# Layer norms of a decoder trunk: row sum taken from the residual addition, variance from a Square on ACT, centred product in PSUM, and the two blocks of the last norm interleaved

## Chip, cores and metric

One core of one Trainium2 chip. The metric is the device time of one execution in microseconds (us). The kernel before has a median of 1365.14 us over three runs (1364.58 to 1365.68).

## The reference, cut to what matters

Two layers over 256 tokens of width 1024, all in float32. Every sublayer is followed by a post-norm residual; there are four of them, numbered 0 to 3 here:

```python
def layer_norm(x, g, b):
    mu = jnp.mean(xf, axis=-1, keepdims=True)
    xc = xf - mu
    var = jnp.mean(xc * xc, axis=-1, keepdims=True)
    y = xc * lax.rsqrt(var + LN_EPS) * g + b

# layer 0
x = layer_norm(DEEP_ALPHA * x + deltanet_mixer(x, ...), ...)         # norm 0
x = layer_norm(DEEP_ALPHA * x + dense_swiglu(x, ...), ...)           # norm 1
# layer 1
x = layer_norm(DEEP_ALPHA * x + sliding_window_mixer(x, ...), ...)   # norm 2
x = layer_norm(DEEP_ALPHA * x + moe_swiglu(x, ...), ...)             # norm 3, the output
```

The last sublayer sends each token to its two best of 8 experts and adds the two results with their weights.

## The kernel before, in words

The 256 tokens are two blocks of 128 (`b` = 0 and 1), one token per partition: the residual `x` is a tile of 128 x 2 x 1024 in SBUF. All large products are made of three float32r matmuls, so every weight unit of 128 x 2048 is first split: SyncE loads it into a ring `raw` of 6 slots, ACT rounds it into `hi` (`cut_hi`, L519), DVE subtracts to get `lo` (`cut_lo`, L832), and TensorE uses it and increments `unit_used`. `hi` and `lo` are rings of 3, so ACT's cut of unit j waits until unit j-3 was used (`AHEAD` = 3). The order of work on each engine is written out by hand, and each engine carries its instructions out in that order; semaphores are all that ties the engines together.

A norm sits between two stages. TensorE ends the projection of block 0 (`block0_done`), then that of block 1 (`unit_used`), into PSUM banks 0 to 3 (norms 0 and 2) or 4 to 7 (norm 1). DVE runs `norm` (L845) for block 0, then for block 1:

```python
step(dve.scalar_tensor_tensor(x = ALPHA * x + ps))                     # L853
link(dve.bn_stats(...)) ; link(dve.bn_stats(...))                      # L857
step(dve.bn_aggr(...)) ; dve.tensor_scalar(lnve = var + 1e-5)          # L859, L860 -> ln_var
step(dve.scalar_tensor_tensor(x = (x - mean) * lng))                   # L864
dve.wait_ge(ln_rstd, ...)                                              # the power -0.5 on POOL, L387
dve.scalar_tensor_tensor(x = x * lnrs + lnb)                           # L867 -> ln_done[b]
```

`step` makes DVE wait for its own instruction, `link` only counts it, `settle` waits for all counted so far. POOL takes `lnve` to the power -0.5 (L387) and, when both blocks of a norm are done, loads the next `lng` and `lnb` (L359, L360). TensorE waits for `ln_done[b]` and transposes the block (`turn_x`, L1286, in `turn`, L1283) into banks 4 to 7; ACT rounds the transposes into `xT_hi` (`turn`, L531, copy at L529), DVE makes `xT_lo` (L842), and the next projection begins.

While this goes on, ACT has only the cuts of the weight units ahead: in norm 0 those of `U_OUT + u + AHEAD` (L664), in norm 1 of `U_DOWN + u + AHEAD` (L681), in norm 2 of `U_O + u + AHEAD` (L740); then it runs `turn`. In norm 2 it also cuts the router weights and issues the DMA that stores each finished block to `xs` in HBM (L748).

Norm 3 comes after the experts. ACT copies the last expert's result out of PSUM and stores it; POOL gathers the two rows of every token with four indirect DMAs (L500) into `picked`; DVE adds them to `x` with four `scalar_tensor_tensor` (L1264: two for block 0, two for block 1) and only then runs `norm(3, None)`, without L853, block 0 and then block 1. SyncE writes each block out once `ln_done[b]` has come (L330). TensorE has nothing left to do there, and after the experts ACT has no work either.

Of the kernel before, what the change touches and what calls it, by code (L numbers as in the profile page):

```python
# [17 lines left out]
ALU = mybir.AluOpType  # L18
# [7 lines left out]
P = 128  # L26
# [6 lines left out]
AHEAD = 3  # L33


def trunk(nc, x_in, w_in, conv_w, a_log, dt_bias, norm_w, w_out, w_kv, w_q, sinks, w_o, w_gu, w_down,
# [39 lines left out]
    with ctx:  # L76
        def sb(name, shape, dt=F32, where=None):
            return (where or ctx).enter_context(nc.sbuf_tensor(name, shape, dt))
# [15 lines left out]
        bnst = sb("bnst", [P, NB, 2, 6])  # L94
        bnmv = sb("bnmv", [P, NB, 2])
# [109 lines left out]
        ln_var, ln_rstd, ln_done = sem("ln_var"), sem("ln_rstd"), [sem(f"ln_done{b}") for b in range(NB)]  # L205
# [312 lines left out]
        def _(act):  # L518
# [16 lines left out]

            act.dma_start(wab[:, :, :], w_in[0][:, QKV * P + D:].rearrange("(k p) n -> p k n", p=P)).then_inc(wab_here, 16)
# [127 lines left out]
            for u in range(4):  # L664
                cut_hi(U_OUT + u + AHEAD)
            turn(2)

# [13 lines left out]
            for u in range(FC):  # L681
                cut_hi(U_DOWN + u + AHEAD)
            turn(3)

# [55 lines left out]
            for u in range(1, 4):  # L740
                cut_hi(U_O + u + AHEAD)
# [7 lines left out]
            turn(4)  # L749
            act.wait_ge(w2_arg, 1)  # L750
# [60 lines left out]
            with act.If(full > P):  # L811
                experts(1)

# [3 lines left out]
        def _(dve):  # L817
# [27 lines left out]
            def norm(i, bank, last=None):  # L845

                for b in range(NB):
                    if bank is not None:
                        if b == 0:
                            dve.wait_ge(block0_done, i + 1)  # L850
                        else:
                            used(last)
                        step(dve.scalar_tensor_tensor(out=x[:, b, :], in0=x[:, b, :], scalar=ALPHA,  # L853
                                                      in1=ps[:, bank + 2 * b:bank + 2 * b + 2, :].rearrange("p b n -> p (b n)"),
                                                      op0=ALU.mult, op1=ALU.add))
                    for q in range(2):
                        link(dve.bn_stats(bnst[:, b, q, :], x[:, b, 512 * q:512 * q + 512]))  # L857
                    settle()
                    step(dve.bn_aggr(bnmv[:, b, :], bnst[:, b, :, :].rearrange("p q s -> p (q s)")))  # L859
                    dve.tensor_scalar(lnve[:, b:b + 1], bnmv[:, b, 1:2], 1e-5, None, ALU.add).then_inc(ln_var, 1)  # L860
                    if b == 0:
                        dve.wait_ge(ln_here, 32 * (i + 1))

                    step(dve.scalar_tensor_tensor(out=x[:, b, :], in0=x[:, b, :], scalar=bnmv[:, b, 0:1], in1=lng[:, :],  # L864
# [842 lines left out]
```

## Time and profile before

| | |
|---|---|
| median of three runs | 1365.14 us |
| lowest, highest | 1364.58, 1365.68 us |
| the profiled execution's own time | 1365.49 us |
| its span in the trace | 1363.7 us |
| busy in the span | PE 93%, PEld 80%, DVE 73%, ACT 60%, POOL 6% |

The span is what the trace covers, from the first instruction to the last. The busy shares are averages over the whole kernel, most of which is the expert stage; what a norm is worth has to be read from the stretch of that norm. PE is TensorE, PEld its weight loads, DVE VectorE, ACT ScalarE, POOL GpSimd, SP SyncE.

### The profile page before, as it was taken

How to read it: one execution, taken by the hardware profiler on the slowest of the kernel's cores; microseconds unless marked ns; L12 is line 12 of the kernel's file. 1: busy time of each engine (PE TensorE's matmuls, PEld its weight loads, DVE VectorE, ACT ScalarE, POOL GpSimd, SP SyncE). 2: the span in 40 equal slices, each digit the busy share in tenths (PEclk: the TensorE clock that was granted, in tenths of full speed). 3: DMA queues.
4: the chain of work that ended last, by engine and by line, in shares of the span. 5: the costliest groups of instructions: out<-in, count | busy, mean ns of one | idle time of the engine just before them, and what ended most of it. 6: DMA issues, size and time to landing. Idle time of an engine off the chain costs nothing.

```text
span 1363.7 us, 18999 instructions
## 1 busy us (share of the span) xinstructions
PE 1262.0 (93%) x6973; PEld 1093.5 (80%) x6973; DVE 1001.4 (73%) x835; ACT 820.7 (60%) x800; POOL 88.2 (6%) x111
## 2 busy tenths in 40 slices
PE   5999988999998977799999999999999999999990
PEld 5997986999986965588888788887788888888880
DVE  4876845455547475388888798888788888888883
ACT  4884342344442463177777777777777777777760
POOL 3033211100002001000000000000000000000001
PEclk8999998999998989599999999999899999999995
DMA  9744011955564423399999999999999999999963
GB/s 315 215 146 133 1 32 62 314 183 185 185 203 146 145 90 105 114 326 367 385 381 353 378 363 379 390 387 343 357 371 382 387 383 353 383 402 373 385 239 110
DMA packets 186522, 366.55 MB, mean 269 GB/s; under 512 B 12192, under 2 KB 69648, under 8 KB 186416
## 3 DMA queue, kind: packets, MB, share of 16 engines
q1 hardware_dynamic: 179744, 345.02, 70.6%
q0 software_dynamic: 4080, 14.80, 3.2%
q10 hardware_dynamic: 2592, 5.36, 1.0%
q8 instruction: 62, 1.02, 0.3%
q14 instruction: 44, 0.36, 0.1%
HBM read 354.65 MB, written 10.49 MB: 268 GB/s over the span
## 4 chain that ended last, share of the span: by engine, by line
PE 86%; DVE 7%; ACT 3%; issue 2%; POOL 1%; DMA 1%; POOLq 0%; SPq 0%; ACTq 0%; DVEq 0%
PE ps L1272 83%; PE ps L1630 1%; DVE lo L834 1%; POOL lnrs L387 1%; DVE conv L895 1%; DVE bnst L857 1%; DVE x L867 1%; DVE xT_lo L842 1%; ACT hi L523 1%; DVE x L853 1%; ACT sS L705 1%; PE ps L1623 0%; DMA picked<-ys,row 0%; DMA x<-in_x 0%; DVE x L1264 0%
## 5 line engine op out<-in xcount | busy, mean ns | idle before, releaser
L834 DVE TENSOR_TENSOR lo<-raw,hi 128x2048 fp32r<-128x2048 f32 x327 | 747.1, 2298 | 197.1 <-ACT hi L523 196.1
L523 ACT ACTIVATE hi<-raw 128x2048 fp32r<-128x2048 f32 x327 | 627.3, 1919 | 363.1 <-PE ps L1272 353.6
L1272 PE MATMUL ps<-hi,xg_hi 128*128 128x512 f32 x704 | 280.8, 399 | 11.0 <-issue 6.3
L1272 PE MATMUL ps<-hi,xg_lo 128*128 128x512 f32 x704 | 276.7, 393 | 0.0
L1272 PE MATMUL ps<-lo,xg_hi 128*128 128x512 f32 x704 | 276.7, 393 | 0.0
L1272 PE MATMUL ps<-xT_hi,hi 128*128 128x256 f32 x624 | 179.9, 288 | 1.3 <-DVE xT_lo L842 1.3
L1272 PE MATMUL ps<-xT_lo,hi 128*128 128x256 f32 x624 | 178.8, 287 | 0.0
L1272 PE MATMUL ps<-xT_hi,lo 128*128 128x256 f32 x624 | 178.7, 286 | 0.0
L1272 PEld LDWEIGHTS ps<-hi,xg_hi 128*128 128x128 f32 x704 | 133.8, 190 | 40.3 <-issue 12.3
L1272 PEld LDWEIGHTS ps<-hi,xg_lo 128*128 128x128 f32 x704 | 133.8, 190 | 28.8
L1272 PEld LDWEIGHTS ps<-lo,xg_hi 128*128 128x128 f32 x704 | 134.0, 190 | 26.9
L1272 PEld LDWEIGHTS ps<-xT_hi,hi 128*128 128x128 f32 x624 | 122.2, 196 | 2.1 <-issue 2.0
L1272 PEld LDWEIGHTS ps<-xT_lo,hi 128*128 128x128 f32 x624 | 122.1, 196 | 0.1
L1272 PEld LDWEIGHTS ps<-xT_hi,lo 128*128 128x128 f32 x624 | 122.1, 196 | 0.0
L1272 PE MATMUL ps<-hi,hE_hi 128*128 128x512 f32 x352 | 110.5, 395 | 0.0
L1272 PE MATMUL ps<-hi,hE_lo 128*128 128x512 f32 x352 | 108.6, 390 | 0.0
L1272 PE MATMUL ps<-lo,hE_hi 128*128 128x512 f32 x352 | 108.5, 389 | 0.0
L1272 PEld LDWEIGHTS ps<-lo,hE_hi 128*128 128x128 f32 x352 | 66.1, 188 | 13.9
L1272 PEld LDWEIGHTS ps<-hi,hE_lo 128*128 128x128 f32 x352 | 66.1, 188 | 13.9
L1272 PEld LDWEIGHTS ps<-hi,hE_hi 128*128 128x128 f32 x352 | 64.3, 188 | 12.1
L482 POOL DMA_INDIRECT xg<-xs,idx x8 | 7.6, 954 | 580.1 <-PE ps L1623 564.4
L895 DVE SCALAR_TENSOR_TENSOR conv<-ps,cw,conv 128x255 f32<-128x255 f32 (+2 forms) x72 | 29.1, 474 | 17.1 <-ACT conv L553 17.1
(270 smaller groups left out, 1244.4 us busy)
## 6 DMA issues: line engine op xcount, KB each, us to landing
raw<-in_moe_w_gu SPq DMA_DIRECT2D x352, 512.0 KB, 6.9
raw<-in_moe_w_down SPq DMA_DIRECT2D x176, 512.0 KB, 5.9
raw<-in_ffn_w_gu SPq DMA_DIRECT2D x44, 512.0 KB, 4.7
raw<-in_dn_w_in SPq DMA_DIRECT2D x32, 512.0 KB, 7.9
raw<-in_ffn_w_down SPq DMA_DIRECT2D x22, 512.0 KB, 4.3
raw<-in_dn_w_out SPq DMA_DIRECT2D x8, 512.0 KB, 4.0
ys<-oneh POOLq DMA_DIRECT2D x1, 4096.0 KB, 16.4
raw<-in_sw_w_q SPq DMA_DIRECT2D x8, 512.0 KB, 4.0
```

The lines of the kernel that those rows point to most:

```text
L387: return pool.tensor_tensor(dst, src, mhalf[:, 0:src.shape[1]], ALU.pow)
L482: pool.indirect_dma_start(xg[:, :], None, xs, bass.IndirectOffsetOnAxis(ap=idx[:, p, e:e + 1], axis=0)).then_inc(gathered, 16)
L523: act.activation(slot(hi, j), slot(raw, j), ACT.Copy).then_inc(hi_ready, 1)
L705: act.activation(s, s, ACT.Exp, bias=nmax[:, st, b, i:i + 1], accum_out=ssum[:, st, b, i:i + 1])
L834: dve.tensor_tensor(slot(lo, j), slot(raw, j), slot(hi, j).bitcast(F32), ALU.subtract).then_inc(lo_ready, 1)
L842: dve.tensor_tensor(xT_part(xT_lo, s), ps[:, 4 + s, :].rearrange("p (k t) -> p k t", k=4), xT_part(xT_hi, s).bitcast(F32), ALU.subtract).t ...
L853: step(dve.scalar_tensor_tensor(out=x[:, b, :], in0=x[:, b, :], scalar=ALPHA, in1=ps[:, bank + 2 * b:bank + 2 * b + 2, :].rearrange("p b n ...
L857: link(dve.bn_stats(bnst[:, b, q, :], x[:, b, 512 * q:512 * q + 512]))
L867: dve.scalar_tensor_tensor(out=x[:, b, :], in0=x[:, b, :], scalar=lnrs[:, b:b + 1], in1=lnb[:, :], op0=ALU.mult, op1=ALU.add).then_inc(ln_ ...
L895: dve.scalar_tensor_tensor(out=conv[:, t, d:T], in0=ps[:, t % 4, 0:T - d], scalar=cw[:, w:w + 1], in1=conv[:, t, d:T], op0=ALU.mult, op1=A ...
L1272: return pe.matmul(dst, lhsT, rhs, start=start, stop=stop)
L1630: last = pe.transpose(ps[:, 6 + c % 2, m * P:(m + 1) * P], actE[:, c % 2, m * P:(m + 1) * P], ident[:, :])
```

## The change

The statistics of a norm are computed in another way. The residual addition also writes out its row sum (`accum_out`), from which DVE makes `lnmu32` = -mean/32 and `lnmu` = mean. ACT computes the Square of x/32 - mean/32 over 1024 columns with a sum, which is the variance (`lnvr`; the squares themselves go to a PSUM region that nobody reads), and adds 1e-5 (`lnve`). POOL's power stays. The centred product goes to PSUM, to the banks of the block's own projection, and the last instruction reads it from there. In ACT's order `deviation` is put between the cuts, before `turn`; one cut of each stage moves to behind `turn`. In norm 3 the additions of the gathered rows become part of `norm`, and the steps of the two blocks alternate.

```diff
+        ln_mean, ln_square = sem("ln_mean"), sem("ln_square")
...
+            def deviation(i, b, bank):
+                act.wait_ge(ln_mean, 2 * i + b + 1)
+                act.activation(ps[:, bank + 2 * b:bank + 2 * b + 2, :].rearrange("p b n -> p (b n)"), x[:, b, :], ACT.Square,
+                               scale=1.0 / 32, bias=lnmu32[:, b:b + 1], accum_out=lnvr[:, b:b + 1]).then_inc(ln_square, 1)
+                act.wait_ge(ln_square, 2 * i + b + 1)
+                act.activation(lnve[:, b:b + 1], lnvr[:, b:b + 1], ACT.Copy, bias=1e-5).then_inc(ln_var, 1)
...
-            for u in range(4):
-                cut_hi(U_OUT + u + AHEAD)
+            cut_hi(U_OUT + 0 + AHEAD)
+            cut_hi(U_OUT + 1 + AHEAD)
+            deviation(0, 0, 4)
+            cut_hi(U_OUT + 2 + AHEAD)
+            deviation(0, 1, 4)
             turn(2)
+            cut_hi(U_OUT + 3 + AHEAD)
...
-            for u in range(FC):
+            for u in range(FC - 2):
                 cut_hi(U_DOWN + u + AHEAD)
+            deviation(1, 0, 0)
+            cut_hi(U_DOWN + FC - 2 + AHEAD)
+            deviation(1, 1, 0)
             turn(3)
+            cut_hi(U_DOWN + FC - 1 + AHEAD)
...
-            for u in range(1, 4):
-                cut_hi(U_O + u + AHEAD)
+            cut_hi(U_O + 1 + AHEAD)
+            deviation(2, 0, 4)
+            cut_hi(U_O + 2 + AHEAD)
+            deviation(2, 1, 4)
...
             turn(4)
+            cut_hi(U_O + 3 + AHEAD)
...
+            for b in range(NB):
+                deviation(3, b, 4)
...
             def norm(i, bank, last=None):
-                for b in range(NB):
+                def pair(bank, b):
+                    return ps[:, bank + 2 * b:bank + 2 * b + 2, :].rearrange("p b n -> p (b n)")
+                def mean(b):
                     if bank is not None:
...
+                        step(dve.scalar_tensor_tensor(out=x[:, b, :], in0=x[:, b, :], scalar=ALPHA, in1=pair(bank, b),
+                                                      op0=ALU.mult, op1=ALU.add, accum_out=lnsum[:, b:b + 1]))
+                    else:
+                        dve.wait_ge(picked_here[b], 32)
+                        step(dve.scalar_tensor_tensor(out=x[:, b, :], in0=picked[:, b, 0, :], scalar=gw[:, b, 2:3],
+                                                      in1=x[:, b, :], op0=ALU.mult, op1=ALU.add))
+                        step(dve.scalar_tensor_tensor(out=x[:, b, :], in0=picked[:, b, 1, :], scalar=gw[:, b, 3:4],
+                                                      in1=x[:, b, :], op0=ALU.mult, op1=ALU.add, accum_out=lnsum[:, b:b + 1]))
+                    dve.tensor_scalar(lnmu32[:, b:b + 1], lnsum[:, b:b + 1], -1.0 / (32 * D), None, ALU.mult).then_inc(ln_mean, 1)
+                    step(dve.tensor_scalar(lnmu[:, b:b + 1], lnsum[:, b:b + 1], 1.0 / D, None, ALU.mult))
-                    for q in range(2):
-                        link(dve.bn_stats(bnst[:, b, q, :], x[:, b, 512 * q:512 * q + 512]))
-                    settle()
-                    step(dve.bn_aggr(bnmv[:, b, :], bnst[:, b, :, :].rearrange("p q s -> p (q s)")))
-                    dve.tensor_scalar(lnve[:, b:b + 1], bnmv[:, b, 1:2], 1e-5, None, ALU.add).then_inc(ln_var, 1)
+                def centre(b):
                     if b == 0:
                         dve.wait_ge(ln_here, 32 * (i + 1))
-                    step(dve.scalar_tensor_tensor(out=x[:, b, :], in0=x[:, b, :], scalar=bnmv[:, b, 0:1], in1=lng[:, :],
+                    link(dve.scalar_tensor_tensor(out=pair(bank or 0, b), in0=x[:, b, :], scalar=lnmu[:, b:b + 1], in1=lng[:, :],
                                                   op0=ALU.subtract, op1=ALU.mult))
+                def finish(b):
+                    settle()
                     dve.wait_ge(ln_rstd, 2 * i + b + 1)
-                    dve.scalar_tensor_tensor(out=x[:, b, :], in0=x[:, b, :], scalar=lnrs[:, b:b + 1], in1=lnb[:, :],
+                    dve.scalar_tensor_tensor(out=x[:, b, :], in0=pair(bank or 0, b), scalar=lnrs[:, b:b + 1], in1=lnb[:, :],
                                              op0=ALU.mult, op1=ALU.add).then_inc(ln_done[b], 1)
+                mean(0)
+                centre(0)
+                if bank is None:
+                    mean(1)
+                    finish(0)
+                else:
+                    finish(0)
+                    mean(1)
+                centre(1)
+                finish(1)
...
             dve.wait_ge(x_scaled, 1)
-            for b in range(NB):
-                dve.wait_ge(picked_here[b], 32)
-                for i in range(2):
-                    step(dve.scalar_tensor_tensor(out=x[:, b, :], in0=picked[:, b, i, :], scalar=gw[:, b, 2 + i:3 + i],
-                                                  in1=x[:, b, :], op0=ALU.mult, op1=ALU.add))
             norm(3, None)
```

## Rows read from the trace of the kernel before

**Rows 1.** The page: its span, and the chain that ended last, by engine.
```profile
span 1363.7 us, 18999 instructions
...
PE 86%; DVE 7%; ACT 3%; issue 2%; POOL 1%; DMA 1%; POOLq 0%; SPq 0%; ACTq 0%; DVEq 0%
```

**Rows 2.** Stretches: length, then busy us (instructions) per engine, PE clock, DMA share, GB/s.
```profile
224.93:237.00 12.07, 6.67 (x33) 5.17 (x32) 10.84 (x15) 4.80 (x4) 3.04 (x2) 0.92 0.26 86
...
1332.00:1363.70 31.70, 0.00 (x0) 0.00 (x0) 13.30 (x16) 0.93 (x1) 6.81 (x6) 0.53 0.32 117
```

**Rows 3.** Timeline of norm 0: start, us, engine, line, operation, shapes [idle before <-releaser].
```profile
224.93 1.22 DVE L853 SCALAR_TENSOR_TENSOR x<-x,ps 128x1024 f32<-128x1024 f32 x1 [1.14 <-PE ps L1272]
...
230.43 1.91 ACT L523 ACTIVATE hi<-raw 128x2048 fp32r<-128x2048 f32 x1 [0.80 <-PE ps L1272]
230.81 1.21 DVE L853 SCALAR_TENSOR_TENSOR x<-x,ps 128x1024 f32<-128x1024 f32 x1
...
233.62 0.15 DVE L860 TENSOR_SCALAR lnve<-bnmv 128x1 f32<-128x1 f32 x1
...
233.85 1.52 POOL L387 TENSOR_TENSOR lnrs<-lnve,mhalf 128x1 f32<-128x1 f32 x1 [4.35 <-DVE lnve L860]
235.48 1.28 DVE L867 SCALAR_TENSOR_TENSOR x<-x,lnrs,lnb 128x1024 f32<-128x1024 f32 x1 [0.51 <-POOL lnrs L387]
...
236.82 1.97 PE L1283 MATMUL ps<-ident,x 128*128 128x128 f32 x8 [4.78 <-DVE x L867]
```

**Rows 4.** Timeline of norm 2: the last instruction of block 1.
```profile
540.63 1.28 DVE L867 SCALAR_TENSOR_TENSOR x<-x,lnrs,lnb 128x1024 f32<-128x1024 f32 x1 [0.87 <-POOL lnrs L387]
```

**Rows 5.** Groups by form: line, engine, operation, shapes, count | busy us, mean ns | idle.
```profile
L853 DVE SCALAR_TENSOR_TENSOR x<-x,ps 128x1024 f32<-128x1024 f32 x6 | 7.3, 1218 | 3.4 <-PE ps L1272 3.4
...
L867 DVE SCALAR_TENSOR_TENSOR x<-x,lnrs,lnb 128x1024 f32<-128x1024 f32 x8 | 10.3, 1284 | 4.5 <-POOL lnrs L387 4.5
...
L1264 DVE SCALAR_TENSOR_TENSOR x<-picked,gw,x 128x1024 f32<-128x1024 f32 x4 | 5.1, 1284 | 18.1 <-DMA picked<-ys,row 18.0
...
L529 ACT ACTIVATE ysb<-ps 128x1024 f32<-128x1024 f32 x8 | 8.1, 1007 | 6.2 <-PE ps L1272 6.2
...
L529 ACT ACTIVATE qT<-ps 128x256 f32<-128x256 f32 x8 | 2.6, 377 | 10.6 <-PE ps L1272 10.6
...
L705 ACT ACT_TABLE_LOAD x1 | 1.3, 1283 | 0.0
...
L707 ACT ACTIVATE ske<-ske 128x8 f32<-128x8 f32 x4 | 0.8, 194 | 0.0
```

**Rows 6.** Timeline: an Exp with a sum on ACT, and a hand-over from DVE to ACT.
```profile
484.26 0.50 ACT L705 ACTIVATE sS<-sS,nmax 128x256 f32<-128x256 f32 x1
484.66 0.19 ACT L705 ACTIVATION_READ_ACCUMULATOR sS<-sS,nmax 128x1 f32 x1
...
553.38 0.16 DVE L1161 TENSOR_TENSOR gw<-m 128x2 f32<-128x2 f32 x1
...
553.58 0.21 ACT L751 ACTIVATE gw<-gw 128x2 f32<-128x2 f32 x1 [9.00 <-DVE gw L1161]
```

**Rows 7.** Timeline of DVE and ACT just after norm 0.
```profile
240.07 4.48 DVE L834 TENSOR_TENSOR lo<-raw,hi 128x2048 fp32r<-128x2048 f32 x2
...
248.10 1.92 ACT L523 ACTIVATE hi<-raw 128x2048 fp32r<-128x2048 f32 x1 [8.67 <-PE ps L1272]
```

**Rows 8.** Timeline of the end of the kernel, norm 3.
```profile
1345.97 5.25 DVE L1264 SCALAR_TENSOR_TENSOR x<-picked,gw,x 128x1024 f32<-128x1024 f32 x4 [17.98 <-DMA picked<-ys,row]
1351.26 1.29 DVE L857 BATCH_NORM_STATS2 bnst<-x 128x6 f32<-128x512 f32 x2
...
1356.02 4.96 SPq L330 DMA_DIRECT2D out<-x  x2
...
1357.70 1.52 POOL L387 TENSOR_TENSOR lnrs<-lnve,mhalf 128x1 f32<-128x1 f32 x1 [3.10 <-DVE lnve L860]
1359.32 1.28 DVE L867 SCALAR_TENSOR_TENSOR x<-x,lnrs,lnb 128x1024 f32<-128x1024 f32 x1 [0.51 <-POOL lnrs L387]
```

More of the change, by code:

```diff
@@ L93, in trunk @@
         mhalf = sb("mhalf", [P, NB * H])
-        bnst = sb("bnst", [P, NB, 2, 6])
-        bnmv = sb("bnmv", [P, NB, 2])
+        lnvr = sb("lnvr", [P, NB])
+        lnsum = sb("lnsum", [P, NB])
+        lnmu = sb("lnmu", [P, NB])
+        lnmu32 = sb("lnmu32", [P, NB])
         lnve = sb("lnve", [P, NB])
@@ L204, in trunk @@
         turned, turn_hi, turn_lo = sem("turned"), sem("turn_hi"), sem("turn_lo")
-        ln_var, ln_rstd, ln_done = sem("ln_var"), sem("ln_rstd"), [sem(f"ln_done{b}") for b in range(NB)]
+        ln_mean, ln_square, ln_var, ln_rstd, ln_done = sem("ln_mean"), sem("ln_square"), sem("ln_var"), sem("ln_rstd"), [sem(f"ln_done{b}") for b in range(NB)]
         conv_step, tap_ready, silu_done = sem("conv_step"), sem("tap_ready"), sem("silu_done")
@@ L852, in norm @@
                             used(last)
-                        step(dve.scalar_tensor_tensor(out=x[:, b, :], in0=x[:, b, :], scalar=ALPHA,
-                                                      in1=ps[:, bank + 2 * b:bank + 2 * b + 2, :].rearrange("p b n -> p (b n)"),
-                                                      op0=ALU.mult, op1=ALU.add))
-                    for q in range(2):
-                        link(dve.bn_stats(bnst[:, b, q, :], x[:, b, 512 * q:512 * q + 512]))
-                    settle()
```

## The prediction

> **What bounds the kernel now.** I read the page first: TensorE holds 86% of the chain that ended last, DVE 7% [rows 1]. So only stretches in which TensorE stands still can give time back, and every norm is one. The stretches by stage come next [rows 2]: the 12.07 us of norm 0 hold 6.67 us of PE work, which lies in their first half, while DVE is busy for 10.84. The last 31.7 us hold no PE work at all, and DVE has the most there, 13.30. Then the timeline of norm 0 [rows 3]. Block 0's addition starts at 224.93, while TensorE is still on block 1. Block 1's starts at 230.81 with no idle time before it, although ACT, released by TensorE, shows that block 1's product was ready by 230.43: DVE, not TensorE, sets that start. From there one chain runs to the transposes at 236.82: addition, statistics, power on POOL, last instruction, 6.0 us in all. Norms 1 and 2 have the same form. In the end stretch [rows 8] the same chain runs twice in a row, behind four additions on DVE, and the output leaves behind it.
>
> **Norms 0 to 2: the statistics.** Before, POOL starts 233.85 - 230.81 = 3.04 us after the addition's start [rows 3]. I build the same distance for the new chain:
> - The addition, 1.22 [rows 5]. Its sum must be read out, for which DVE shows no row. Bounds: nothing (hidden under the pipeline), or a small DVE instruction of its own, 0.15 [rows 3]. I take 0.08, since such an instruction overlaps its predecessor on ACT by half [rows 6].
> - 0.03 for DVE's wait for itself, 0.15 for `lnmu32` [rows 3], 0.04 to hand over to ACT (553.38 + 0.16 to 553.58) [rows 6]. `lnmu` comes after it and lies beside ACT.
> - The Square over 1024 columns. Lower end 1.01, the copy of 1024 columns [rows 5]. Upper end: an Exp with a bias per partition and a sum takes 0.50 for 256 columns [rows 6] where a copy takes 0.38 [rows 5], so 1.01 + 0.12 = 1.13. I take 1.12, since it has bias and sum. The read of the sum starts 0.10 before its end and takes 0.19 [rows 6]: 0.09 more. Together 1.21, between 1.10 and 1.22.
> - 0.03 for ACT's wait for itself, 0.20 for `lnve` (a small ACT instruction, 0.19 [rows 5] to 0.21 [rows 6]), and 0.08 to POOL (233.62 + 0.15 to 233.85) [rows 3].
>
> Sum: 1.22 + 0.08 + 0.03 + 0.15 + 0.04 + 1.21 + 0.03 + 0.20 + 0.08 = 3.04, with ends 2.84 and 3.12. So the chain stays as long as it was: what DVE saves in two BATCH_NORM_STATS2 comes back as a Square with two hand-overs. Per block the difference is 0.0 (-0.2 to +0.1), and six blocks are in a row on the path (block 0 delays block 1, since DVE sets its start): 0.0, between -1.2 and +0.5.
>
> The **Trainium skill** (VectorE: DVE Perf Modes, "Two Vector instructions with no wait between them") says that an op which also writes its accumulator is two instructions. By that the read-out is certainly there, but no row here prices it.
>
> **Centred product in PSUM.** The last instruction then reads PSUM. The addition with its PSUM source takes 1218 ns and the last instruction with none 1284 [rows 5], but the first also has a constant for its scalar where the other reads one per partition. So I take 1.28 for both new forms; the end below is 1.22 for each last instruction, -0.06 for six blocks, -0.4. The centring lies under the wait for POOL: it now starts some 0.1 later and still ends over 1 us before the power does.
>
> **Queues passed.** On ACT block 0's `deviation` comes before the third cut, which TensorE releases about 2.8 us after the addition's start; it is about over by then, so that cut moves by a few tenths. Block 1's comes before `turn`, so block 0's `xT_hi` copies move back by some 1.5 us, to before DVE wants them (behind its last instruction). The fourth cut (230.43) moves to after `turn`, to about 239.4 to 241.4. DVE's second subtraction behind `turn` wants it 2.2 us into the pair that starts at 240.07 [rows 7], some 0.9 later; TensorE wants it after two more units, and the first is only used up at 248.10 [rows 7]. Cost 0. Without that cover it would be up to 1.9 per norm (the cut). Norm 1 is alike. In norm 2 the fourth cut comes before the small Exp of the routing, but only just behind `turn`, which has 6 us and more before that Exp. The store of block 0 to `xs` is queued behind block 1's `deviation`, but the gathers wait for both stores, and block 1's stays where it is. SyncE refills `raw` when `lo` is made, in DVE's unchanged order; POOL's loads of `lng` wait for the same `ln_done`. Nothing moves.
>
> One accident: in norm 2 block 1's last instruction sat idle for 0.87 us before it [rows 4] where 0.51 is usual [rows 3]. I can't tell what of; if it goes, -0.36.
>
> **Norm 3.** Before: additions at 1345.97 (1.32 each with their waits), statistics at 1351.26, last instruction of block 1 1359.32 to 1360.60 [rows 8]. After, with the durations above:
> - Block 0's two additions end at 1348.57, its `lnmu32` starts at 1348.71; `lnmu`, then the centring from 1348.95 to 1350.23.
> - Block 1's additions follow from 1350.15; the second ends at 1352.75 and `lnmu32` starts at 1352.86.
> - Block 0's power is over at 1348.71 + 0.15 + 0.04 + 1.21 + 0.03 + 0.20 + 0.08 + 1.53 = 1351.95, hidden under those additions. Its last instruction runs 1353.1 to 1354.4, centring of block 1 to 1355.6.
> - Block 1's power ends at 1352.86 + 1.71 + 1.53 = 1356.10; hand-over 0.1 (233.85 + 1.52 to 235.48) [rows 3]; last instruction 1356.2 to 1357.5.
>
> So 1360.6 - 1357.5 = 3.1 us, with ends of 2.8 and 3.5 by the bounds. The first output transfer starts at about 1354.4 instead of 1356.02, the second 3.1 us behind it; from the last instruction's end to the end of the span it was 1363.7 - 1360.6 = 3.1, and I leave that.
>
> **Sum.** 1365.49 (the profiled execution) - 3.1 - 0.0 = 1362.4. That execution lies 0.35 above the median of 1365.14, so for a median: **1362.0**. 0.2% is 2.7 us, about what a measurement can tell here from no change.
>
> **Rivals.**
> - **A, the statistics get shorter too (0.15).** The lower ends (Square near 1.01, read-outs hidden, PSUM reads at 1.22) and the stall of norm 2 gone: 0.1 to 0.2 per block. For it: every bound is of this trace. Time 1361.0.
> - **B, the summing addition runs slower (0.07).** The four additions of `picked` read both tensors from SBUF at 1284 ns for 1024 columns [rows 5], and none writes a sum. If a sum cost such an instruction its rate, the two that make one would take about 1.07 more each, and both are on the path in norm 3: 2.1 of 3.1 lost, 1364.1. In norms 0 to 2 one tensor is in PSUM, so nothing changes there. The Trainium skill (Vector Engine (DVE) Microarchitecture Reference, "Points that are easy to get wrong") says that a scalar_tensor_tensor with two non-bf16 SBUF sources halves throughput, none being left for the accumulator. The rows show no halving without a sum; whether there is one with it no row tells.
> - **C, Square is not in the table that Exp leaves behind (0.08).** Elsewhere Square follows Silu, with no load of its own; in norm 2 it follows the Exps, loaded at L705, 1283 ns a load [rows 5]. A load in front of block 0's Square is 1.3 on the path; the one back for the routing's Exp lies mostly beside TensorE's work. Time 1363.4.
> - **D, the detour over ACT is longer than the sum says, and the kernel is slower (0.02).** ACT would wait until the Square's writes have landed before the sum can be read and handed on. It is on the path six times in norms 0 to 2; in norm 3 it eats into the 3.1 only once (block 0's is hidden for 1.1 us). It decides from 3.1 / 7 = 0.44 us per block on; at 0.9 it gives 1362.0 + 6.3 = 1368.3. Against it: the read of a sum starts 0.10 before its Exp ends [rows 6].
> - That the change doesn't do what it says is hardly open: the interleaved order is in DVE's own queue.
>
> **How the numbers follow.** The forecast has 0.68, A 0.15, B 0.07, C 0.08, D 0.02. The forecast's own range is 1361.3 to 1362.9 (0.5 either way for six small terms, 0.3 for norm 3). For 8 in 10 I take A in and reach to C: 1360.8 to 1363.6. Faster by over 0.2% means under 1362.4: A, and about two thirds of the forecast, 0.60. Same: its rest, B and C, 0.38. Slower: D, 0.02.
>
> **What would show it.** Right: POOL's power starts 2.9 to 3.1 us after each addition's start; norms 0 to 2 keep their 6.0 us from block 1's addition to the transposes; in the end stretch no idle time on DVE before block 0's last instruction, under 1 us before block 1's, and 11.5 us from the first addition to the last instruction's end instead of 14.6. Wrong: an L523 cut that the subtraction behind `turn` waits for; an ACT_TABLE_LOAD in norm 2; summing additions over 1.5 us; a power that starts over 3.3 us after the addition.

## Result, and the profile after

The changed kernel takes 1356.59 us (median of 6 runs, 1355.35 to 1358.09) beside 1365.35 for the kernel before (6 runs, 1364.58 to 1366.37). The ratio is 0.9936, 95% interval [0.9923, 0.9949]: 8.8 us faster, where 3.1 were forecast. The direction was right, and the time lies well below the range.

The profiled execution took 1356.62. The page of the changed kernel gives the span and the chain, and the stretches of norm 0 and of the end follow in the columns of [rows 2].

```profile
span 1354.8 us, 19018 instructions
...
PE 88%; DVE 5%; ACT 3%; issue 2%; DMA 1%; POOL 1%; POOLq 0%; SPq 0%; ACTq 0%; DVEq 0%
```

```profile
225.16:237.30 12.14, 7.98 (x40) 6.63 (x38) 9.24 (x14) 6.21 (x10) 2.28 (x5) 0.89 0.26 86
1326.00:1354.80 28.80, 0.03 (x1) 0.00 (x0) 10.55 (x14) 3.91 (x7) 6.62 (x6) 0.57 0.36 129
```

DVE's share of the chain falls from 7 to 5%. In norm 0 DVE is busy for 9.24 us in place of 10.84 [rows 2], and ACT, with its two Squares, for 6.21 in place of 4.80.

To find the 8.8 us I cut both spans at the same events: the start of each norm's first addition, and the end of its last instruction. This table is worked out from the timelines of DVE and ACT; "experts" ends where ACT, its last `ysb` copy done, issues that copy's store, and "gathers" ends with the first addition of `picked`.

| part, us | before | after | difference |
|---|---|---|---|
| up to norm 0 | 224.93 | 225.16 | +0.23 |
| norm 0 | 11.83 | 10.38 | -1.45 |
| feed-forward | 186.67 | 185.49 | -1.18 |
| norm 1 | 11.85 | 10.37 | -1.48 |
| attention | 94.43 | 94.48 | +0.05 |
| norm 2 | 12.20 | 10.39 | -1.81 |
| experts | 791.04 | 790.91 | -0.13 |
| gathers | 13.02 | 13.22 | +0.20 |
| norm 3 | 14.63 | 11.32 | -3.31 |
| output | 3.10 | 3.08 | -0.02 |

The sum is -8.90, the difference of the spans. Norm 3 gave what was forecast (3.31 for 3.1). Norms 0 to 2, put at 0.0, gave 4.74. The four norms together make 8.05; of the rest the largest part is the 1.18 of the feed-forward stage, which is taken up again below. The timeline of norm 0 after shows where (start, us, engine, line, operation, shapes, idle before it and its releaser):

```profile
228.17 0.55 POOL L389 TENSOR_TENSOR lnrs<-lnve,mhalf 128x1 f32<-128x1 f32 x1 [25.30 <-ACT lnve L543]
228.82 1.28 DVE L898 SCALAR_TENSOR_TENSOR x<-ps,lnrs,lnb 128x1024 f32<-128x1024 f32 x1 [0.85 <-POOL lnrs L389]
...
230.60 1.22 DVE L878 SCALAR_TENSOR_TENSOR x<-x,ps 128x1024 f32<-128x1024 f32 x1 [0.50 <-PE ps L1309]
231.75 0.08 DVE L878 DVE_READ_ACCUMULATOR x<-x,ps 128x1 f32 x1
231.87 0.15 DVE L886 TENSOR_SCALAR lnmu<-lnsum 128x1 f32<-128x1 f32 x1
...
232.05 1.12 ACT L540 ACTIVATE ps<-x,lnmu 128x1024 f32<-128x1024 f32 x1 [2.16 <-DVE lnmu L886]
232.12 1.29 DVE L892 SCALAR_TENSOR_TENSOR ps<-x,lnmu,lng 128x1024 f32<-128x1024 f32 x1
233.11 0.19 ACT L540 ACTIVATION_READ_ACCUMULATOR ps<-x,lnmu 128x1 f32 x1
233.33 0.20 ACT L543 ACTIVATE lnve<-lnvr 128x1 f32<-128x1 f32 x1
...
233.61 0.55 POOL L389 TENSOR_TENSOR lnrs<-lnve,mhalf 128x1 f32<-128x1 f32 x1 [4.89 <-ACT lnve L543]
234.26 1.28 DVE L898 SCALAR_TENSOR_TENSOR x<-ps,lnrs,lnb 128x1024 f32<-128x1024 f32 x1 [0.85 <-POOL lnrs L389]
```

The new chain from the addition to POOL's start is 233.61 - 230.60 = 3.01 us; it was put at 3.04, and it was 3.04 before [rows 3]. What changed is the instruction behind it. POOL's power, the same operation on the same 128x1 tile, takes 0.55 us where it took 1.52 [rows 3]. From block 1's addition to the end of its last instruction that makes 234.26 + 1.28 - 230.60 = 4.94 us in place of 235.48 + 1.28 - 230.81 = 5.95.

Block 0 gets less of it. Its last instruction starts 3.66 us after its addition where it took 4.68 before, but block 1's addition comes only 5.44 after block 0's instead of 5.88, and now it shows 0.50 us of idle time released by TensorE. Before it had none [rows 3]. Block 0 gives 0.44 and block 1 1.01, together the 1.45 of norm 0.

The end of the changed kernel, in the same columns:

```profile
1340.40 1.28 DVE L882 SCALAR_TENSOR_TENSOR x<-picked,gw,x 128x1024 f32<-128x1024 f32 x1 [18.19 <-DMA picked<-ys,row]
...
1344.50 1.28 DVE L882 SCALAR_TENSOR_TENSOR x<-picked,gw,x 128x1024 f32<-128x1024 f32 x1
...
1344.79 1.42 POOL L389 TENSOR_TENSOR lnrs<-lnve,mhalf 128x1 f32<-128x1 f32 x1 [6.53 <-ACT lnve L543]
1345.82 1.28 DVE L884 SCALAR_TENSOR_TENSOR x<-picked,gw,x 128x1024 f32<-128x1024 f32 x1
...
1348.65 1.28 DVE L892 SCALAR_TENSOR_TENSOR ps<-x,lnmu,lng 128x1024 f32<-128x1024 f32 x1
1348.76 3.33 SPq L332 DMA_DIRECT2D out<-x  x2
1348.89 1.45 POOL L389 TENSOR_TENSOR lnrs<-lnve,mhalf 128x1 f32<-128x1 f32 x1 [2.67 <-ACT lnve L543]
1350.44 1.28 DVE L898 SCALAR_TENSOR_TENSOR x<-ps,lnrs,lnb 128x1024 f32<-128x1024 f32 x1 [0.51 <-POOL lnrs L389]
```

Here the power takes 1.42 and 1.45 again. So its time depends on what runs beside it. Each long power has a DVE instruction that reads two tensors from SBUF, started before the power did, and ends 0.40 to 0.43 us after that instruction's end:

- before, block 1 of norm 0: the centring (233.69, 1.28 us) ends at 234.97, the power (233.85, 1.52) at 235.37;
- after, norm 3: the addition of `picked` 1344.50 + 1.28 = 1345.78, the power 1344.79 + 1.42 = 1346.21; the centring 1348.65 + 1.28 = 1349.93, the power 1348.89 + 1.45 = 1350.34.

In norms 0 to 2 after, the centring is over (232.12 + 1.29 = 233.41) before the power starts at 233.61.

The row of before that shows this best wasn't among the ones I had chosen. It is the centring in block 1 of norm 0:

```profile
233.69 1.28 DVE L864 SCALAR_TENSOR_TENSOR x<-x,bnmv,lng 128x1024 f32<-128x1024 f32 x1
```

### The profile page after: what moved, and what is told of

It is laid out like the page before. It is cut to its first block, busy times and chain, and to the rows that moved or that the text cites. A ratio compares the mean times of both kernels' runs of the same rounds, so it can differ in the third digit from the quotient of the medians.

```text
span 1354.8 us, 19018 instructions
## 1 busy us (share of the span) xinstructions
PE 1261.9 (93%) x6973; PEld 1094.1 (81%) x6973; DVE 991.2 (73%) x827; ACT 831.3 (61%) x824; POOL 82.0 (6%) x111
## 4 chain that ended last, share of the span: by engine, by line
PE 88%; DVE 5%; ACT 3%; issue 2%; DMA 1%; POOL 1%; POOLq 0%; SPq 0%; ACTq 0%; DVEq 0%
PE ps L1309 85%; PE ps L1667 1%; DVE lo L856 1%; DVE conv L937 1%; ACT hi L525 1%; ACT sS L722 1%; PE ps L1320 0%; PE ps L1660 0%; DMA picked<-ys,row 0%; DVE xT_lo L864 0%; DMA x<-in_x 0%; DVE x L898 0%; ACT ps L540 0%; DMA ys<-ysb 0%; ACT ps L574 0%
```

## The experiments

The theory: a power of POOL that starts while DVE works through an instruction with two SBUF inputs is held until that is done (called P or the hold in the expectations); without it the power takes 0.55. The rival: the power waits for what was written by DVE, and is quick when ACT wrote its input (W). Runs of one batch share the runs of before beside them, and those medians lie between 1365.47 and 1366.22.

**1. The kernel before, centring behind the power.** `ln_rstd` is waited for first.

```diff
+                    dve.wait_ge(ln_rstd, 2 * i + b + 1)
                     step(dve.scalar_tensor_tensor(out=x[:, b, :], in0=x[:, b, :], scalar=bnmv[:, b, 0:1], in1=lng[:, :],
                                                   op0=ALU.subtract, op1=ALU.mult))
-                    dve.wait_ge(ln_rstd, 2 * i + b + 1)
```

> Theory P (shared reads): POOL's power takes 1.52 us in the kernel before because DVE's centring, which reads two tensors from SBUF, runs at the same time, and the power cannot read its one input until the centring is over; alone it takes 0.55. Here the centring of the kernel before waits for the power. P expects 0.55 per power in all eight, and a kernel that is only some 2 to 3 us slower than before (the centring's 1.28 comes onto the path, 0.97 leaves it, 0.3 per block). Rival W (who wrote the input): a power whose input DVE has written takes 1.52 and one whose input ACT has written takes less; it expects 1.52 here and about 10 us more.

One run: 1367.04, before 1366.22. The timeline of norm 0 in this kernel:

```profile
235.38 0.55 POOL L387 TENSOR_TENSOR lnrs<-lnve,mhalf 128x1 f32<-128x1 f32 x1 [5.67 <-DVE lnve L860]
235.97 1.28 DVE L865 SCALAR_TENSOR_TENSOR x<-x,bnmv,lng 128x1024 f32<-128x1024 f32 x1 [0.67 <-POOL lnrs L387]
```

All eight powers take 0.55 to 0.57, norm 3's too, though DVE still writes their input: W is out. The time gains nothing, since 1.28 of centring is now on the path for 0.97 saved, 0.31 a block (norm 0: 12.46, 0.63 longer). The 2 to 3 us of loss that I expected don't show in this one time. In its trace the four norms are 2.85 us longer, 0.68 of which is a wait of norm 3 for the gathered rows of block 1, which the first trace of before doesn't have; the feed-forward and attention stages are shorter (185.90 and 93.27).

**2. The kernel before, sum left in PSUM.** In norms 0 to 2 the addition writes to PSUM, and statistics and centring read it there. The centring then has one SBUF input, `lng`, and still runs beside the power.

```diff
-                        step(dve.scalar_tensor_tensor(out=x[:, b, :], in0=x[:, b, :], scalar=ALPHA,
-                                                      in1=ps[:, bank + 2 * b:bank + 2 * b + 2, :].rearrange("p b n -> p (b n)"),
+                        src = ps[:, bank + 2 * b:bank + 2 * b + 2, :].rearrange("p b n -> p (b n)")
+                        step(dve.scalar_tensor_tensor(out=src, in0=x[:, b, :], scalar=ALPHA,
+                                                      in1=src,
                                                       op0=ALU.mult, op1=ALU.add))
...
-                        link(dve.bn_stats(bnst[:, b, q, :], x[:, b, 512 * q:512 * q + 512]))
+                        link(dve.bn_stats(bnst[:, b, q, :], src[:, 512 * q:512 * q + 512]))
...
-                    step(dve.scalar_tensor_tensor(out=x[:, b, :], in0=x[:, b, :], scalar=bnmv[:, b, 0:1], in1=lng[:, :],
+                    step(dve.scalar_tensor_tensor(out=x[:, b, :], in0=src, scalar=bnmv[:, b, 0:1], in1=lng[:, :],
```

> The kernel before with one difference: in norms 0 to 2 the residual sum is left in PSUM, so that the statistics and the centring read it there, and the centring has a single SBUF input; nothing is computed on ACT. P expects the powers of norms 0 to 2 at 0.55 although the centring still runs beside them, those of norm 3 (unchanged) at 1.52, the last instruction bound by the centring's end, 0.35 to 0.45 earlier per block, and the kernel at 1362.5 to 1363.5, 2 to 3 us under before. W expects 1.52 in all eight, since DVE still writes the input, and no change in the time.

1360.97 (1359.5 to 1361.56), ratio 0.9963 [0.9949, 0.9977]. The timeline of norm 0 and of norm 3 in this kernel:

```profile
229.71 1.27 DVE L867 SCALAR_TENSOR_TENSOR x<-ps,bnmv,lng 128x1024 f32<-128x1024 f32 x1
229.88 0.55 POOL L387 TENSOR_TENSOR lnrs<-lnve,mhalf 128x1 f32<-128x1 f32 x1 [25.51 <-DVE lnve L863]
...
1348.56 1.54 POOL L387 TENSOR_TENSOR lnrs<-lnve,mhalf 128x1 f32<-128x1 f32 x1 [9.50 <-DVE lnve L863]
```

The centring starts 0.17 us before the power and runs for 1.27, and the power is over in 0.55. In norm 3, where `x` stays in SBUF, it takes 1.54. So a busy DVE isn't enough; it takes the second SBUF input. Norms 0 to 2 take 10.94, 10.94 and 10.93, 3.07 less than before in all, as expected. The median falls by 5.25 and lies 1.5 below the expected stretch. In the trace the feed-forward stage is 1.26 shorter than in the first trace of before; what else makes the difference stays open.

**3. The changed kernel, centring held back to the power's start.**

```diff
+                    if bank is not None:
+                        dve.wait_ge(ln_var, 2 * i + b + 1)
                     link(dve.scalar_tensor_tensor(out=pair(bank or 0, b), in0=x[:, b, :], scalar=lnmu[:, b:b + 1], in1=lng[:, :],
```

> The kernel after with one wait more: in norms 0 to 2 the centring waits until ACT has made POOL's input, so it starts when the power does. P expects powers of 1.4 to 1.5 in norms 0 to 2 and a kernel at 1361 to 1363: 1.1 per block, less the 0.5 of slack that block 1 has now against TensorE. W expects powers of 0.55, with the last instruction waiting for the centring instead (0.6 per block), 1358.5 to 1359.5.

1359.16 (1358.68 to 1361.03), ratio 0.9952 [0.9935, 0.9969]. The powers of norms 0 to 2 stay at 0.55, not the 1.4 to 1.5 I expected. The timeline of norm 0 in this kernel:

```profile
228.95 0.55 POOL L389 TENSOR_TENSOR lnrs<-lnve,mhalf 128x1 f32<-128x1 f32 x1 [25.31 <-ACT lnve L543]
229.00 1.29 DVE L894 SCALAR_TENSOR_TENSOR ps<-x,lnmu,lng 128x1024 f32<-128x1024 f32 x1 [1.58 <-ACT lnve L543]
```

`ln_var` releases both, and POOL starts 0.05 us earlier (0.02 to 0.06 in the six of norms 0 to 2). My theory had only said "beside", and by itself this run fits W, which had expected 0.55 and 1358.5 to 1359.5. But W is out by experiment 1, and by norm 3 of the changed kernel, where ACT writes the power's input and it takes 1.42 and 1.45. So the theory had to be sharpened: whichever of the two starts first decides, and experiment 4 tries that. The centring, 1.29, isn't slower for it. The lesser gain comes from the centring, which now starts later and ends after the power (norm 0: 11.22).

**4. The same, with the wait that lets the centring start first.** `ln_square` in place of `ln_var`.

```diff
+                    if bank is not None:
+                        dve.wait_ge(ln_square, 2 * i + b + 1)
                     link(dve.scalar_tensor_tensor(out=pair(bank or 0, b), in0=x[:, b, :], scalar=lnmu[:, b:b + 1], in1=lng[:, :],
```

> The kernel after; in norms 0 to 2 the centring waits until the Square is done, one small ACT instruction before POOL's input is there, so it starts 0.2 to 0.25 us ahead of the power, where in the run before it started 0.05 us behind it and the powers took 0.55. P (the start decides) expects the powers of norms 0 to 2 at 1.40 to 1.50, the last instruction 4.65 us after the addition's start instead of 3.66, norms of 11.8 to 11.9 us as in the kernel before, and 1361 to 1363. If the earlier run means that the centring never holds a power whose input ACT wrote, they stay at 0.55 and the kernel is at 1359.

1361.66 (1359.97 to 1363.05), ratio 0.9971 [0.9961, 0.9981]. The timeline of norm 0 in this kernel:

```profile
228.86 1.29 DVE L894 SCALAR_TENSOR_TENSOR ps<-x,lnmu,lng 128x1024 f32<-128x1024 f32 x1 [1.34 <-ACT ps L540]
229.04 1.51 POOL L389 TENSOR_TENSOR lnrs<-lnve,mhalf 128x1 f32<-128x1 f32 x1 [25.41 <-ACT lnve L543]
```

Now the centring starts 0.18 us ahead of the power, and the power takes 1.51; the six of norms 0 to 2 take 1.49 to 1.53. Beside the changed kernel again (1357.18 in this batch) 4.5 us are given back, nearly all that norms 0 to 2 had brought; in the traces these norms take 4.35 more. This is the hold's price in the changed kernel.

**5. The changed kernel, norm 3's blocks in turn.**

```diff
-                if bank is None:
-                    mean(1)
-                    finish(0)
-                else:
-                    finish(0)
-                    mean(1)
+                finish(0)
+                mean(1)
                 centre(1)
```

> The kernel after with the two blocks of norm 3 one after the other. P expects the powers of norm 3 at 0.55, since nothing with two SBUF inputs is beside them, 12.3 us from the first addition's start to the last instruction's end where the interleaved order has 11.3, so 1357.6: the interleaving is worth 1.0 us only, the rest of the end's 3.3 us is the statistics. The reckoning of my prediction (a power of 1.53 throughout) expects 14.3 us and 1359.6. On the time that the feed-forward stage gained (1.18 us between norm 0 and norm 1, with TensorE's clock back at full speed after 13 matmuls at half speed instead of 26): norms 0 to 2 are those of the kernel after here, so if the length of TensorE's stand in norm 0 decides it, this run shows 185.4 us again; if it is a matter of when the chip looks, it may show any value from 185.4 to 186.6.

1358.13 (1356.69 to 1359.22), ratio 0.9948 [0.9932, 0.9965]. The powers of norm 3 take 0.57 and 0.55, and norm 3 takes 12.58, 1.26 more than interleaved. So of norm 3's 3.31 us only 1.26 are the interleaving's; 2.05 come with the new statistics and two powers that are not held (2 x 0.97 = 1.94).

**6. The changed kernel, in norm 3 the second centring before the first last instruction.**

```diff
                 if bank is None:
                     mean(1)
+                    centre(1)
                     finish(0)
                 else:
                     finish(0)
                     mean(1)
-                centre(1)
+                    centre(1)
                 finish(1)
```

> The kernel after, in norm 3 with block 1's centring ahead of block 0's last instruction instead of behind it. The second batch's picture is: a power is held only by a DVE instruction that reads two tensors from SBUF and has started before it (theory P, sharpened: the start decides). Block 1's centring is then over before block 1's power starts (at about +8.5 us from the first addition), and what runs beside the power is block 0's last instruction, which reads PSUM and one tensor of SBUF. P expects block 1's power at 0.55 instead of 1.45, block 0's still at 1.4, 10.6 to 10.8 us for norm 3 instead of 11.3, and 0.3 to 0.7 us less in all if the two output transfers, now 1.2 us apart instead of 3.0, don't get in each other's way. If any DVE instruction beside it held the power, block 1's would stay at 1.4 and nothing be won.

1357.71 (1355.4 to 1358.42), ratio 0.9938 [0.9924, 0.9952]. The timeline of norm 3 in this kernel, the last instructions of both blocks in one row (1.28 for the first), then block 1's power:

```profile
1350.21 2.48 DVE L898 SCALAR_TENSOR_TENSOR x<-ps,lnrs,lnb 128x1024 f32<-128x1024 f32 x2
1350.37 0.55 POOL L389 TENSOR_TENSOR lnrs<-lnve,mhalf 128x1 f32<-128x1 f32 x1 [2.67 <-ACT lnve L543]
```

Block 1's power falls from 1.45 to 0.55 and norm 3 from 11.32 to 10.80, as the start rule says. Here a DVE instruction of the same length starts 0.16 us ahead of the power and doesn't hold it: it reads one tensor from SBUF (`lnb`) and one from PSUM, like the centring of experiment 2. The total can't be told from the changed kernel's 1357.18. No kernel that I ran is measurably faster than the changed one.

**7 and 8. Both kernels once more, in the batch of 4 and 6.**

> The kernel after, unchanged, for the same chip as the two above and for a second profile. P expects the same powers (0.55 in norms 0 to 2, 1.4 in norm 3) and norms of 10.4 us. The 1.18 us that the stage between norm 0 and norm 1 gained in the first profile came with TensorE's clock back after 14 matmuls at half speed instead of 27. If that belongs to the change, this profile shows 14 and 185.5 us again; if it depends on when the chip looks, the count may be anything between 13 and 27.

> The kernel before, unchanged, for a second profile. P expects powers of 1.52 in all eight and norms of 11.85 us. The stage between norm 0 and norm 1 (186.67 us in the first profile) may be anything from 185.4 to 186.7 if the clock's return is a matter of when the chip looks. The last instruction of norm 2's block 1, which came 0.36 us late in the first profile, comes late again if that belongs to the kernel.

The changed kernel: 1357.18 (1356.46 to 1357.74), ratio 0.9937 [0.9924, 0.9951]; powers 0.55 and, in norm 3, 1.42 and 1.45. The kernel before, one run: 1363.59, beside 1365.81 for its other runs; norms 11.83, 11.85, 12.20 and powers 1.52 to 1.54 as in the first trace. Its norm 3 takes 14.79, since DVE waits 0.19 for the gathered rows of block 1; in experiments 1 and 2 that wait is 0.68 and 0.67. In the interleaved order no trace shows it, because block 0's centring comes between the additions.

**9. The kernel before with only norm 3 as changed.** This is meant to price norm 3 alone (the diff shows its core; `deviation` and `end_norm` are the changed kernel's functions).

```diff
         bnmv = sb("bnmv", [P, NB, 2])
+        lnvr = sb("lnvr", [P, NB])
+        lnsum = sb("lnsum", [P, NB])
+        lnmu = sb("lnmu", [P, NB])
+        lnmu32 = sb("lnmu32", [P, NB])
...
+            for b in range(NB):
+                deviation(3, b, 4)
...
-            norm(3, None)
+            end_norm(3, None)
```

> The kernel before with norm 3 alone done as in the kernel after (sum from the second addition, Square on ACT, centred product in PSUM, the two blocks interleaved); norms 0 to 2 and ACT's order in them stay as before. This is the part that my prediction had counted on: theory P expects powers of 1.52 in norms 0 to 2 and norms of 11.85 us there, 1.4 in norm 3, 11.3 us from the first addition to the last instruction's end instead of 14.6, and 3.3 us less than before in all, 1362.5. If the parts were not additive (the end drawing on what norms 0 to 2 do), the total would be off that by more than 1 us. A rival on the size of the change, that it comes from moving the cuts on ACT, expects nothing here beyond the 3.3 either, but was to show in the runs with the centring held, which keep the moved cuts and lost 4 us.

1373.44 (1372.79 to 1376.42), ratio 1.0062 [1.0048, 1.0075]: 8 us slower than before, where 3 faster were expected. Norm 3 does what it should, 11.32 us. The loss is in the experts' stage, 803.08 us in place of 791.04, and there in TensorE's 512-column matmuls: in 300 us of it 1325 records stand where before has 1364 (some records can be missing, but experiments 11 and 12 show the same). This kernel's instructions on TensorE are those of before. What differs is where tiles lie: the four new ones push all later tiles along in SBUF.

**10 to 12. The place of the tiles.** In 10 the four tiles of experiment 9 are allocated behind all others. In 11 the kernel before has one unused tile. In 12 the changed kernel has one.

```diff
         token = sb("token", [P, NB])
+        lnvr = sb("lnvr", [P, NB])
+        lnsum = sb("lnsum", [P, NB])
+        lnmu = sb("lnmu", [P, NB])
+        lnmu32 = sb("lnmu32", [P, NB])
```

```diff
         bnmv = sb("bnmv", [P, NB, 2])
+        room = sb("room", [P, 8])
```

```diff
         lnmu32 = sb("lnmu32", [P, NB])
+        room = sb("room", [P, 28])
```

> The kernel before with the changed end alone, as in the run that came out 8 us slower than before (1373.4), where the groups of 48 matmuls of the experts took 11.20 us in place of 10.93. The one edit against that run: the four small tiles (32 bytes a partition together) are allocated behind all other tiles, so that no other tile lies elsewhere than in the kernel before. Theory S (the place of the tiles in SBUF sets the matmuls' pace): the experts' groups of 48 take 10.93 again, the stage from norm 2 to the last expert 791 us, and the time is that of the end's saving, 1365.3 - 3.3 = 1362.0, range 1361 to 1363.5. Rival N (the program's size, its extra semaphores, or where the instructions lie): these are as in the slow run, so 11.20 for 48 matmuls, and 1373 again.

> The kernel before with one unused tile of 32 bytes a partition behind bnmv: every later tile lies 32 bytes further, no instruction differs otherwise. Theory S (place in SBUF): groups of 48 matmuls of the experts at 11.20 us, the expert stage about 802 us, and the time 1365.3 + 11.3 = 1376.6, range 1374 to 1379. Rival N (program, semaphores): 1365.3, as before. A third possibility, that the pace differs by chance from one built program to the next, gives one or the other here without regard to the place, and shows itself if this run and the one beside it disagree with theory S in either direction.

> The changed kernel with one unused tile of 112 bytes a partition behind its four new small tiles: later tiles then lie 32 bytes further than in the kernel before, in place of 80 bytes nearer. Theory S: the matmuls slow as in the run with the changed end alone, the expert stage about 802 us, and the time 1357.0 + 11.3 = 1368.3, range 1366 to 1371. Rival N: 1357, as the changed kernel. In either case POOL's power stays 0.55 us in norms 0 to 2 and these norms 10.4 us.

The sizes in these expectations are wrong in one respect: every tile gets whole places of 32 bytes a partition, as the built programs' lists of addresses show. `xT_hi` starts at byte 132992 in the kernel before, and also in the changed one (its six small tiles fill just the 192 bytes that the four of before did) and in experiment 10; at 133024 in 11; at 133120 in 9 and 12.

| kernel | later tiles moved by | median, us | ratio | experts, us |
|---|---|---|---|---|
| 9: end only | 128 bytes | 1373.44 | 1.0062 [1.0048, 1.0075] | 803.08 |
| 10: end only, tiles last | 0 | 1361.38 | 0.9972 [0.9961, 0.9983] | 790.99 |
| 11: before, 32 bytes of room | 32 bytes | 1377.22 | 1.0083 [1.0068, 1.0098] | 807.32 |
| 12: changed, 112 bytes of room | 128 bytes | 1372.32 | 1.0051 [1.0037, 1.0065] | 807.37 |

The stretch 960:1260 of the kernels before, 10, 11 and 12, in this order, in the columns of [rows 2]. The second number is PE's busy time with its matmul records:

```profile
960.00:1260.00 300.00, 300.00 (x1364) 247.94 (x1363) 261.05 (x148) 226.10 (x154) 1.87 (x2) 1.00 1.02 376
```

```profile
960.00:1260.00 300.00, 300.00 (x1362) 247.83 (x1362) 260.42 (x148) 225.55 (x154) 1.88 (x2) 1.00 1.02 376
```

```profile
960.00:1260.00 300.00, 299.18 (x1324) 241.88 (x1325) 253.89 (x145) 221.19 (x152) 1.88 (x2) 0.99 1.01 370
```

```profile
960.00:1260.00 300.00, 299.93 (x1324) 243.11 (x1325) 253.18 (x145) 220.35 (x151) 1.88 (x2) 0.99 1.01 369
```

PE is busy nearly all the time and the granted clock is 0.99 to 1.00, yet 3% fewer matmuls are done. The timeline of TensorE in the kernel before, then in 11, shows the step from one 512-column matmul to the next, 0.227 us (six steps in 1.36) and 0.233 (six in 1.40):

```profile
1000.06 0.39 PE L1272 MATMUL ps<-hi,xg_hi 128*128 128x512 f32 x1
...
1001.42 0.39 PE L1272 MATMUL ps<-hi,xg_hi 128*128 128x512 f32 x1
```

```profile
999.71 0.40 PE L1273 MATMUL ps<-hi,xg_hi 128*128 128x512 f32 x1
...
1001.11 0.40 PE L1273 MATMUL ps<-hi,xg_hi 128*128 128x512 f32 x1
```

Experiment 11 settles that the place does it, since no instruction of it differs otherwise, and 10 undoes it with the instructions of 9. The weight tiles `raw`, `hi` and `lo` are allocated ahead of the small tiles and haven't moved: of a 512-column matmul of the experts only the operand made from the tokens (`xg_hi`, `xg_lo`, `hE_hi`, `hE_lo`) lies elsewhere, and with it the tiles that other engines use meanwhile. Experiment 12 came out 4.0 us above its expected 1368.3. Both 9 and 12 have the later tiles at the same addresses, and the experts' stage differs by 4.3; between 900 and 1000 us the clock is 1.00 in 9 and 0.97 in 12, with 434 and 422 matmul records, 12 steps of 0.233 or 2.8 us of it. In 11 the feed-forward stage takes 184.29 (before 186.67) and attention 92.83 (94.43), the shortest of all traces; in 9 and 12, moved by 128, the two stages take 187.81 and 93.51, and 185.29 and 94.53, so whether a move can also help is open. Which tile's place counts wasn't tried, nor any other distance.

## Why the prediction was wrong, step by step

- **What bounds the norms: right.** DVE's chain set the end of every norm. That block 0 passes on a gain only until TensorE sets block 1's start was not said, since no gain was forecast there. It limits block 0 to 0.44 of about 1.0 us.
- **Addition to POOL, 3.04 us: right, 3.01 in the trace.** Its terms came out too: addition 1.22, sum read-out 0.08 (mostly beside the addition), `lnmu32` 0.15, Square 1.12, its read-out 0.19, `lnve` 0.20.
- **The failed step** is what stands under "Centred product in PSUM", and with it the term of norms 0 to 2, 0.0, which measured 4.74. The prediction said of the centring that it "lies under the wait for POOL", and so cost it at nothing. I had asked what covers the centring, but not what the centring does to POOL, which waits under it. The power was carried over at its duration of before, and that duration is 0.55 of its own and 0.97 of hold by the centring. In the new chain the centring no longer waits for the variance. In block 1 of norm 0 it starts 232.12 - 230.60 = 1.52 us after the addition, beside the Square, where before it was 233.69 - 230.81 = 2.88; the prediction's "it now starts some 0.1 later" was wrong. It is over 0.20 us before the power starts. Had the prediction set the centring's end against the power's start, and not against its end, this would have shown. Five numbers confirm it: 0.55 when the centring is moved away (1), 0.55 when it has one SBUF input (2), 0.55 when POOL starts 0.05 first (3), 1.51 when DVE starts 0.18 first (4), and 4.5 us given back by that wait alone.
- **The Trainium skill had the rule**, and I had not weighed it: SBUF — State Buffer, "Who interferes with whom", says that a DVE instruction with two SBUF inputs contends with a GpSimd instruction that reads SBUF, and that the order of issue decides who is held. The traces here agree where DVE starts first, and they price it at 0.97 us a power. Where POOL starts first, by 0.02 to 0.06 us in experiment 3, it isn't held, which agrees too, but DVE isn't seen to be held either (1.29).
- **Norm 2's 0.36 us: gone, as its accident was priced.** Norm 2 gives 1.81 where norms 0 and 1 give 1.45 and 1.48. The idle time of 0.87 [rows 4] shows up in every trace in which norm 2's power was held, in experiment 4 too (0.86), and in none with a free power. Why norm 2 alone has it stays open.
- **Norm 3, 3.1 us: right, 3.31, in part by luck.** The prediction's 1.53 for both powers was nearly met (1.42 and 1.45) only because in the interleaved order another DVE instruction with two SBUF inputs starts just ahead of each, of which the prediction says nothing. And it laid nearly the whole 3.1 on the interleaving, with the statistics at 0.0, where experiment 5 gives the interleaving 1.26. The kernel with this part alone (10) came out at 1361.38, 4.2 below its neighbours (the interval of its ratio is 2.3 to 5.3 us); in its trace norm 3 gives 3.31. The hold of 1.42 beside block 1's additions was hidden, as predicted; block 1's, 1.45 in place of 1.53, was on the path.
- **Queues passed, 0: right.** The attention and experts' stages agree within 0.13 us, and DVE's subtractions behind `turn` run without a wait for the moved cut. The feed-forward stage is 1.18 shorter, by the clock. After norm 0 TensorE starts at a granted clock of 0.50 (the 1.2 GHz level) and comes back to 1.00. In the profiled run of before 27 matmuls of 256 columns run at the lower level, in that of after 14; their steps are 0.215 and 0.12 us, so 13 x 0.095 = 1.2. The prediction has no term for this. It is hardly chance: over all traces the count is 20 to 27 in the six in which norm 0 takes 11.7 to 11.8 us (before, before again, experiments 4, 9, 10 and 11) and 12 to 18 in the five in which it takes 10.4 to 10.5 (after, after again, 5, 6 and 12). With the tiles at their places the stage takes 186.43 us on average in the kernels with the norms of before (before, before again and 10) and 185.68 in those with the changed ones (after, after again, 5 and 6). These 0.75 us and the norms' 8.05 make 8.80, which fits the medians (8.76). Why is not shown: experiments 1, 2 and 3, with norms of 12.5, 10.9 and 11.2, have 19, 13 and 26 (the stage takes 186.60 in the third), so the norm's length alone doesn't set it. The stretches of 4 us behind the transposes, of before and then of after:

```profile
239.44:243.44 4.00, 4.00 (x19) 4.00 (x20) 3.98 (x3) 0.00 (x0) 3.06 (x7) 0.50 0.91 348
243.44:247.44 4.00, 4.00 (x28) 4.00 (x28) 1.11 (x1) 0.00 (x0) 0.00 (x0) 0.77 1.01 349
```

```profile
238.22:242.22 4.00, 4.00 (x22) 4.00 (x23) 3.98 (x3) 1.78 (x1) 3.06 (x7) 0.61 0.93 340
242.22:246.22 4.00, 4.00 (x36) 4.00 (x35) 1.11 (x1) 0.52 (x1) 0.00 (x0) 1.00 1.00 348
```

- **Rival A** expected gains in norms 0 to 2, but from the statistics, which got no shorter (3.04 to 3.01). Its price of 0.1 to 0.2 a block is far from the 0.44 and 1.01 measured. **B** is out: the summing addition of `picked` takes 1.28 (L884), as the one without a sum (L882); the halving that the prediction quotes isn't there. **C** is out: no table load stands before a Square, and there are 19 in the groups by form, as before. **D** is out: from Square's start to POOL's 1.56 us where 1.52 was reckoned.

## What to carry to other kernels

Before a duration is carried over to a changed kernel, ask what ran beside it: a 128x1 operation that takes 1.52 us is a reason to look for the instruction whose end it follows. A DVE instruction with two SBUF inputs is best started after, not shortly before, a small POOL instruction on the critical path, or given one input in PSUM. Compare the addresses of the big tiles, or the step of the matmuls in a distant stage, before a difference is put down to an edit: 32 bytes of an unused tile cost 12 us here, more than the whole change brought.

## What the runs showed of the hardware that was not expected

- **Who starts first decides.** POOL's power (128x1) takes 0.55 to 0.57 us alone, 0.55 to 0.56 when it starts 0.02 to 0.06 before DVE's two-input instruction, and 1.42 to 1.54 when it starts 0.16 to 0.30 after it; then it ends 0.40 to 0.44 after DVE's. DVE isn't slowed in any of these (1.27 to 1.29). A DVE instruction with one input in PSUM that starts 0.16 or 0.17 ahead doesn't hold the power (0.55 to 0.56).
- **The place of tiles changes the matmuls' pace.** At full granted clock, with the same instructions, the step of a 512-column matmul is 0.227 us with the later tiles at one place and 0.233 with them 32 or 128 bytes further, and the experts' stage 791 or 803 to 807 us.
- **A sum costs DVE nearly nothing.** The read-out is a row of its own (DVE_READ_ACCUMULATOR, 0.08 us) that starts 0.07 before the addition's end, also with both inputs in SBUF.
